# Norms: sums completed by VectorE, four tiles centred and the odd low halves made by GpSimd

## The reference

```
def layer_norm(x, g, b):
    mu = mean(x);  xc = x - mu;  var = mean(xc * xc)
    return xc * rsqrt(var + 1e-5) * g + b

# first block, layer 0 and 1
x = layer_norm(ALPHA * x + 0.5 * swiglu(x, w_in, w_out))      # norms out0, out2
x = layer_norm(ALPHA * x + mix)                               # rg_out (recurrence), o (attention)
x = layer_norm(ALPHA * x + 0.5 * swiglu(x, w_in, w_out))      # norms out1, out3
# second block
h = layer_norm(concat(meta, x))                               # norm emb
h = layer_norm(ALPHA * h + mix);  h = layer_norm(ALPHA * h + swiglu(h))   # mixo0, out4, mixo1, out5
```

## Time and profile before

| | before |
|---|---|
| median of three runs | 1757.0 us (1755.71 to 1757.52) |
| the profiled execution | 1757.72 us, its span 1755.9 us |
| TensorE busy | 1723.1 us (98%), granted clock 0.99 |
| VectorE busy | 1241.3 us (71%) |
| ScalarE busy | 972.5 us (55%) |
| GpSimd busy | 0.2 us, 4 instructions (memsets of one column) |
| DMA, share of the 16 engines | 49.2% |

### The profile page before, as it was taken

The page is one execution under the profiler, slowest core; times in us unless marked ns, Lnnn a source line. Parts: engine busy times, 40 slices in busy tenths (PEclk is TensorE's granted clock), DMA queues, the critical chain, the costliest instruction groups (busy, mean ns, idle before and its releaser), DMA issues.

```text
span 1755.9 us, 33282 instructions
## 1 busy us (share of the span) xinstructions
PE 1723.1 (98%) x11772; PEld 1566.7 (89%) x11772; DVE 1241.3 (71%) x2175; ACT 972.5 (55%) x1700; POOL 0.2 (0%) x4
## 2 busy tenths in 40 slices
PE   8999998999999999999899999999999999999998
PEld 7888998888899888888788888989999999898887
DVE  6776789777664776677787766868665567787765
ACT  5564596655455655466565544565534346665543
POOL 0000000000000000000000000000000000000000
PEclk9999999999999999999999999999999999999999
DMA  6555355455544656533265563334455534345562
GB/s 225 191 201 194 132 181 181 143 186 200 192 142 157 202 186 218 162 116 123 87 217 191 184 213 133 101 117 132 148 175 188 184 114 132 115 145 191 191 203 85
DMA packets 76349, 288.80 MB, mean 164 GB/s; under 512 B 9312, under 2 KB 11616, under 8 KB 76256
## 3 DMA queue, kind: packets, MB, share of 16 engines
q1 hardware_dynamic: 76256, 287.53, 49.2%
HBM read 286.45 MB, written 1.05 MB: 164 GB/s over the span
## 4 chain that ended last, share of the span: by engine, by line
PE 92%; DVE 5%; ACT 2%; issue 1%; DMA 0%; SPq 0%; ACTq 0%; DVEq 0%
PE psum L526 33%; PE psum L527 17%; PE psum L518 12%; PE psum L520 11%; PE psum L519 11%; PE psum L657 1%; PE psum L769 1%; PE psum L604 1%; DVE wlo L1542 1%; PE psum L652 1%; DVE r_sq L1706 1%; ACT whi L1077 1%; PE psum L871 0%; DVE r_sq L1738 0%; PE psum L943 0%
## 5 line engine op out<-in xcount | busy, mean ns | idle before, releaser
L1542 DVE TENSOR_TENSOR wlo<-raw,whi 128x1024 fp32r<-128x1024 f32 (+2 forms) x494 | 640.7, 1305 | 281.2 <-ACT whi L1077 279.9
L526 PE MATMUL psum<-x_split,whi 128*128 128x512 f32 x1760 | 618.4, 395 | 4.3 <-DVE x_split L1577 3.1
L1077 ACT ACTIVATE whi<-raw 128x1024 fp32r<-128x1024 f32 (+2 forms) x494 | 544.8, 1116 | 37.8 <-PE psum L520 18.7
L527 PE MATMUL psum<-x_split,wlo 128*128 128x256 f32 x1760 | 494.5, 281 | 0.0
L526 PEld LDWEIGHTS psum<-x_split,whi 128*128 128x128 f32 x1760 | 331.5, 188 | 82.1 <-DVE x_split L1577 2.8
L518 PE MATMUL psum<-x_split,whi 128*128 128x272 f32 (+1 forms) x1168 | 342.1, 293 | 3.9 <-DVE x_split L1743 3.8
L520 PE MATMUL psum<-x_split,wlo 128*128 128x272 f32 (+1 forms) x1168 | 333.8, 286 | 0.0
L519 PE MATMUL psum<-x_split,whi 128*128 128x272 f32 (+1 forms) x1168 | 332.9, 285 | 0.0
L527 PEld LDWEIGHTS psum<-x_split,wlo 128*128 128x128 f32 x1760 | 331.8, 189 | 0.0
L526 PE MATMUL psum<-h_split,whi 128*128 128x512 f32 x770 | 272.2, 397 | 0.0
L518 PEld LDWEIGHTS psum<-x_split,whi 128*128 128x128 f32 x1168 | 220.2, 189 | 11.4 <-issue 6.3
(11 more groups left out here) (226 smaller groups left out, 1655.7 us busy)
## 6 DMA issues: line engine op xcount, KB each, us to landing
raw<-w_in SPq DMA_DIRECT2D x264, 512.0 KB, 3.3
raw<-w_out SPq DMA_DIRECT2D x96, 704.0 KB, 4.2
raw<-w_mix SPq DMA_DIRECT2D x42, 512.0 KB, 3.3
raw<-w_rg SPq DMA_DIRECT2D x25, 512.0 KB, 3.8
raw<-w_q SPq DMA_DIRECT2D x24, 512.0 KB, 3.3
raw<-w_kv SPq DMA_DIRECT2D x16, 512.0 KB, 3.3
raw<-w_mixo SPq DMA_DIRECT2D x16, 512.0 KB, 3.2
raw<-w_rg_out SPq DMA_DIRECT2D x8, 640.0 KB, 3.9
```

What stands on the lines that cost most here:

```text
L526: nc.tensor.matmul(ps[:, bank, :], whi[slot][:, w], split, start=start, stop=False)
L527: return nc.tensor.matmul(part(bank, 0), wlo[slot][:, w], split[:, 0], start=False, stop=stop)
L1077: nc.scalar.activation(whi[slot][:, 0:cols], raw[slot][:, 0:cols], ACT.Copy).then_inc(w_hi_done, count)
L1542: V.tensor_tensor(wlo[slot][:, 0:cols], raw[slot][:, 0:cols], f(whi[slot][:, 0:cols]), ALU.subtract).then_inc(w_lo_done, 1)
```

## The change

The sums. VectorE itself adds the eighth tile, first its values and then its squares (two instructions of T columns), so that `sums` is complete; TensorE makes the means from `sums` alone, half as many matmuls of both kinds. The low half of the third chunk, which VectorE made at this place, is GpSimd's now. TensorE fills with seven matmuls while the sums are completed. The mean's square no longer waits for the mean of the squares.

The centring. TensorE makes the mean a second time (PSUM bank 3), ScalarE copies it to SBUF (`prod`), and GpSimd centres tiles 4 and 5, then 6 and 7 from that copy. VectorE keeps 0 to 3.

The low halves. VectorE makes those of the even tiles. For an odd tile ScalarE writes the shifted value a second time, unrounded, into `sq`, and GpSimd subtracts the high half from it. `first_chunks` waits for one semaphore or the other by turns. In norm emb only this last part applies.

The one-column Sqrt with its table load moves from the end of the stage to its last four chunks or its fifth.

```diff
@@ -552,3 +560,7 @@
             for k in range(KD):
-                pe.wait_ge(x_ready, KD * x_of[st.name] + k + 1)
+                others = KD // 2 * (x_of[st.name] - 1) + k // 2 + 1
+                if k % 2:
+                    pe.wait_ge(x_odd_ready, others)
+                else:
+                    pe.wait_ge(x_ready, KD + others)
                 for j in range(FIRST):
...
@@ -669,18 +679,22 @@
                     pe.wait_ge(sq_done, KD * n + k + 1)
-                    token_means(sq[:, k, :], 4)
+                    token_means(sq[:, k, :], 5, k == 0, False)
                 pe.wait_ge(emb_squares, 1)
-                ins = token_means(sums[:, 1, :], 4, True)
+                ins = token_means(sums[:, 1, :], 5, False)
             else:
-                pe.wait_ge(sums_done, norm_stages.index(name) + 1)
-                means(sums[:, 0, :], first=True)
-                token_means(sums[:, 0, :], 0)
-                token_means(sums[:, 1, :], 4)
-                pe.wait_ge(acc_free, by_name[name].u0 + by_name[name].units)
-                means(r[:, KD - 1, :], last=True).then_inc(mean_done, 1)
-                token_means(r[:, KD - 1, :], 0)
-                pe.wait_ge(sq_done, KD * (n + 1))
-                ins = token_means(sq[:, KD - 1, :], 4, True)
+                ns = norm_stages.index(name)
+                pe.wait_ge(ax_shifted, (KD - 1) * (ns + 1))
+                keep_warm(7)
+                pe.wait_ge(values_summed, ns + 1)
+                means(sums[:, 0, :], True, True).then_inc(mean_done, 1)
+                token_means(sums[:, 0, :], 2).then_inc(value_means, 1)
+                pe.wait_ge(squares_summed, ns + 1)
+                ins = token_means(sums[:, 1, :], 5)
             ins.then_inc(stat_done, 1)
-            keep_warm(6)
+            if name == "emb":
+                keep_warm(6)
+            else:
+                nc.tensor.matmul(acc(3, T), ones_d, sums[:, 0, t], start=True, stop=True).then_inc(mean_again, 1)
+                keep_warm(3)
             pe.wait_ge(rstd_done, n + 1)
@@ -691,2 +705,5 @@
             keep_warm(12)
+            if name != "emb":
+                pe.wait_ge(mean_copied, norm_stages.index(name) + 1)
@@ -1061,2 +1078,28 @@
+    @block.gpsimd
+    def _(pool):
+        for name in norm_stages:
+            if by_name[name].next:
+                n, slot, _, cols = ahead(by_name[name].next, 0, 0)
+                pool.wait_ge(w_lo_done, n)
+                pool.wait_ge(w_hi_done, n + 1)
+                nc.gpsimd.tensor_tensor(wlo[slot][:, 0:cols], raw[slot][:, 0:cols], whi[slot][:, 0:cols].bitcast(fp32),
+                                        ALU.subtract).then_inc(w_lo_done, 1)
+            T = tokens[name]
+            t = slice(tok0(T), TOK)
+            odd = "emb" if name == "out3" else name
+            pool.wait_ge(mean_copied, norm_stages.index(name) + 1)
+            for k in (4, 6):
+                mean = prod[:, 0, t].unsqueeze(1).broadcast_to([P, 2, T])
+                nc.gpsimd.tensor_tensor(r[:, k:k + 2, t], r[:, k:k + 2, t], mean, ALU.subtract).then_inc(pool_centred, 1)
+            if odd in version:
+                T = norms[norm_no[odd]][1]
+                t = slice(tok0(T), TOK)
+                for k in range(1, KD, 2):
+                    pool.wait_ge(x_hi_done, KD * version[odd] + k + 1)
+                    pool.wait_ge(odd_moved, KD // 2 * (version[odd] - 1) + k // 2 + 1)
+                    nc.gpsimd.tensor_tensor(x_lo[:, k, t], sq[:, k, t], x_hi[:, k, t].bitcast(fp32),
+                                            ALU.subtract).then_inc(x_odd_ready, 1)
     @block.scalar
@@ -1104,5 +1147,8 @@
-        def before_norm(st):
+        def root_table():
             nc.scalar.activation(spare[:, :], eps[:, :], ACT.Sqrt)
+        def before_norm(st):
             if st.next:
@@ -1166,2 +1212,4 @@
                 round_ahead(so, i, j)
+                if isinstance(i, int) and SLOTS * i + j == so.chunks - SLOTS:
+                    root_table()
                 if j % 2:
@@ -1189,2 +1237,4 @@
                 round_ahead(st, i, j)
+                if m == SLOTS:
+                    root_table()
                 if m:
@@ -1206,12 +1256,15 @@
                 for k in range(KD):
-                    act.wait_ge(xc_done, 4 * n + k // 2 + 1)
+                    act.wait_ge(xc_done, xc_before(n) + k // 2 + 1)
                     nc.scalar.activation(sq[:, k, :], r[:, k, :], ACT.Square).then_inc(sq_done, 1)
-            act.wait_ge(stat_done, n + 1)
             if name == "emb":
-                nc.scalar.activation(std_t[:, 0:nt], ps[:, 5, 4:4 + nt], ACT.Sqrt, bias=eps[:, 0:1]).then_inc(std_done, 1)
+                act.wait_ge(stat_done, n + 1)
+                nc.scalar.activation(std_t[:, 0:nt], ps[:, 5, 0:nt], ACT.Sqrt, bias=eps[:, 0:1]).then_inc(std_done, 1)
             else:
                 ns = norm_stages.index(name)
-                nc.scalar.activation(msq[:, 0:nt], ps[:, 5, 0:nt], ACT.Square).then_inc(msq_done, 1)
+                act.wait_ge(value_means, ns + 1)
+                nc.scalar.activation(msq[:, 0:nt], ps[:, 2, 0:nt], ACT.Square).then_inc(msq_done, 1)
                 act.wait_ge(var_ready, ns + 1)
                 nc.scalar.activation(std_t[:, 0:nt], var_t[:, 0:nt], ACT.Sqrt, bias=eps[:, 0:1]).then_inc(std_done, 1)
+                act.wait_ge(mean_again, ns + 1)
+                nc.scalar.activation(prod[:, 0, t], acc(3, T), ACT.Copy).then_inc(mean_copied, 1)
             nxt = None if name == "out3" else by_name["out3" if name == "emb" else name].next
@@ -1224,2 +1277,4 @@
                     nc.scalar.activation(x_hi[:, k, t], r[:, k, t], ACT.Identity, bias=b(k)).then_inc(x_hi_done, 1)
+                    if k % 2:
+                        nc.scalar.activation(sq[:, k, t], r[:, k, t], ACT.Identity, bias=b(k)).then_inc(odd_moved, 1)
                 else:
@@ -1671,5 +1726,3 @@
                 dve.wait_ge(sq_done, i + (KD * norm_no[st.name] + j))
-                ins = V.tensor_tensor(sums[:, :, t], sums[:, :, t], r_sq[:, :, i + (j - 1), t], ALU.add)
-                if last:
-                    ins.then_inc(sums_done, 1)
+                V.tensor_tensor(sums[:, :, t], sums[:, :, t], r_sq[:, :, i + (j - 1), t], ALU.add)
@@ -1685,5 +1738,8 @@
                 V.tensor_copy(sums[:, :, t], r_sq[:, :, 0, t])
-            if last and st.next:
+            if last:
-                rest_of_chunk(*ahead(st.next, 0, 0))
+                dve.wait_ge(acc_free, st.u0 + st.units)
+                V.tensor_tensor(sums[:, 0, t], sums[:, 0, t], r[:, m, t], ALU.add).then_inc(values_summed, 1)
+                dve.wait_ge(sq_done, KD * (norm_no[st.name] + 1))
+                V.tensor_tensor(sums[:, 1, t], sums[:, 1, t], sq[:, m, t], ALU.add).then_inc(squares_summed, 1)
@@ -1722,3 +1778,4 @@
                 dve.wait_ge(msq_done, ns + 1)
-                V.tensor_tensor(var_t[:, 0:nt], ps[:, 5, 4:4 + nt], msq[:, 0:nt], ALU.subtract).then_inc(var_ready, 1)
+                dve.wait_ge(stat_done, n + 1)
+                V.tensor_tensor(var_t[:, 0:nt], ps[:, 5, 0:nt], msq[:, 0:nt], ALU.subtract).then_inc(var_ready, 1)
             dve.wait_ge(std_done, n + 1)
@@ -1727,11 +1784,8 @@
                 centre(2)
-                centre(4)
             dve.wait_ge(spread, n + 1)
-            dve.wait_ge(xc_done, 4 * n + 3)
+            dve.wait_ge(xc_done, xc_before(n + 1))
             v = version.get(name, 0)
             for k in range(KD + 1):
-                if k == 2 and name != "emb":
-                    centre(6)
-                if k == 6:
-                    dve.wait_ge(xc_done, 4 * n + 4)
+                if k in (4, 6) and name != "emb":
+                    dve.wait_ge(pool_centred, 2 * norm_stages.index(name) + k // 2 - 1)
                 if k < KD:
@@ -1739,3 +1793,3 @@
                                            acc(6, T), ALU.mult, ALU.mult).then_inc(xn_done, 1)
-                if k and kind == "x":
+                if k % 2 and kind == "x":
                     c = C_B + KD * n + k - 1
@@ -1747,2 +1801,4 @@
                 if nxt:
+                    dve.wait_ge(w_lo_done, nxt.n0 + 3)
                     rest_of_chunk(*ahead(nxt, 0, 1))
```

20 lines of the change are left out of this document (13 added, 7 removed).

## The result

| | before | after |
|---|---|---|
| median | 1757.0 us (1755.36 to 1758.13, 9 runs) | 1761.8 us (1759.93 to 1763.41, 9 runs) |
| the profiled execution | 1757.72 us, its span 1755.9 us | 1762.68 us, its span 1760.9 us |
| TensorE busy | 1723.1 us | 1718.5 us, granted clock 0.99 |
| VectorE busy | 1241.3 us | 1231.0 us |
| ScalarE busy | 972.5 us | 987.6 us |

The ratio is 1.0029 (95% interval 1.0021 to 1.0037): slower, by 4.8 us. I had forecast 1743, faster. The rival B, an exclusion of VectorE and GpSimd, had 1762.

A forecast was written before the change was run, and what follows sets the result against it. Behind the norms, head and loop were taken as bound by the norm's own chain and VectorE's pace. Norm gains of 15.2 us, less 1.2 for GpSimd hand-overs, gave 14.0 off: 1743 us, range 1737 to 1762.

The forecast's parts named there:

- rival B: VectorE and GpSimd exclude each other when both read two operands in SBUF: +5 us, 1762; chance 0.37.
- GpSimd's chunk low half leaves VectorE for nothing here: Head behind out0: moving this subtraction to GpSimd changes nothing, since it stood in VectorE's wait for the mean.
- The reciprocal at 3.3: Behind out0: reciprocal 3.3 us after the last product's start, before 3.59.
- The first scaling at 4.25: Behind out0: first scaling 4.25 us after the last product's start, before 5.06; later than 4.4 means the head was misread.
- The first product at 5.9: Behind out0: next stage's first product 5.9 us after the last product's start, before 6.75.
- The loop 6.2 to 6.4: Behind out0: the stretch in which eight tiles arrive takes 6.2 to 6.4 us, before 6.73.
- The circle: In the loop: low half, scaling, rounding, low half with two hand-overs, the longest path, 1.45 us per pair of tiles.
- GpSimd's price: In centrings and odd low halves: 2.6 ns a column from the scan, 1.34 us per pair of tiles, 0.67 per tile.
- C: No change, about 1757 us: no exclusion, but GpSimd at about 4 ns a column, so the loop's loss eats the head's gain; chance 0.16.
- The statistics of 272 tokens: Behind mixo0 and out4: twelve of 24 one-column matmuls gone, 1.3 us less about 0.3; those norms gain 2.2 and 2.4.
- Out5: Norm out5, without halves: scaling 0.81 us earlier and the centring behind it gone, taken as 1.15 us gained.

The follow-up runs named there:

- The probe: Kernel before, with GpSimd instructions and overlapping VectorE ones appended behind its end: VectorE's 256-column SBUF subtraction 2.54 us against 0.42 with a PSUM operand; kernel time meaningless.
- the kernels with the early copy: Changed kernel, chunk low halves at norm's end behind an added wait, mean copied from the first mean's bank: 1750.7 us; all tile low halves on VectorE: 1748.3.
- the split kernel: Against the 1748.3 us kernel (mean copied early, all low halves on VectorE): in seven stages 512 third-chunk columns moved into VectorE's wait for the mean; 1744.6 us, 0.9933.

## Why the prediction was wrong

**The step that failed** is "GpSimd's chunk low half leaves VectorE for nothing here", and behind it the choice that GpSimd's instructions run beside VectorE's at no cost to either. In its place the runs showed an exclusion: the chunk's low half holds VectorE's sums (2.65 us for 0.69 behind out0, 2.12 for 0.42 behind o), and the kernel is 8.3 us faster with it off GpSimd; VectorE's chunk work holds GpSimd's last odd low half (1.30 for 0.73), and the kernel is 5.4 us faster without that hold. I had the rule in hand and gave it 0.37. What spoke against it was only that no row showed GpSimd at work; that is no evidence, and the difference between operands in SBUF and in PSUM was readable in every row of VectorE. The Trainium skill has it right (SBUF — State Buffer, section "Who interferes with whom"): two SBUF inputs of VectorE against a read of GpSimd, held for the whole instruction. The probe agrees: 2.54 us against 0.42.

**Point by point.**
- The reciprocal at 3.3: 3.75 after. With the chunk's low half off GpSimd 3.37. The step was right but for GpSimd.
- The first scaling at 4.25: 4.72 after (201.67). 0.38 of it is the late sums (3.75 against 3.37); the spread stays last, as I had it.
- The first product at 5.9: 7.13. Of the 1.2 us, 0.38 is the late sums, 0.72 the first low half held by the second centring. In the kernels with the early copy it is 6.26, with 0.23 of it for the wait ahead of the first centring.
- The loop 6.2 to 6.4: 6.81. The circle was well estimated: 6.25 once the last odd low half is not held.
- GpSimd's price, 1.34 and 0.67 us from the scan: 1.26 and 0.72 alone. C, which wanted 4 ns a column, is out. The Trainium skill's 4497 ns for 2048 columns (GPSIMD Engine Reference, section 3.1) fits the runs: 0.72, 1.26 and 2.34 us for 256, 512 and 1024 lie on a line of 0.18 us and 2.11 ns a column, which gives 4.50 there.
- The statistics of 272 tokens: behind out4 the clock is 1.00 instead of 0.67, and 1.2 came in although the last low half was held; 2.44 in the split kernel, where I had 2.4.
- Out5: 1.04 to the end of the span, where I had 1.15.
- Rival B: three norms +0.8 (measured 0.46), rg_out +1.3 (0.84), mixo1 and o +1.8 (2.30, 2.46), mixo0 +0.9 (0.46), out4 and emb -0.7 together, out3 and out5 -2.3. Its sum of +5 was right, but by luck as to its terms, of which three were not: I had the chunk's low half end before the last product behind out0 to out2, without harm, but it holds the last addition of 512 columns and so that of the eighth tile (0.40); I had not seen that VectorE's chunk work holds GpSimd's last low half (0.56 in each of nine norms); and I had each even low half of the loop meet an odd one, 0.35 per pair, but behind out0 only the first is held, and the others keep 0.48 to 0.49.

**The accounting.** From the changed kernel's 1761.8 us, the holds are undone one at a time: the added wait at the end of the loop gives 5.4 us (1756.4), the chunk back on VectorE 8.3 (1753.5). They do not add: with both it is 1755.3, where the third chunk's low half is late. With the centrings early and the chunk divided 1744.6 is reached, 12 less than before and next to the forecast's 14 less; that the two are so close is in part luck, since behind o 1.23 came in for 2.0 and behind out3 with emb 1.80 for 1.45, at granted clocks of 0.79 and 0.91. So the gain that I forecast was there to be had, from the shorter head and the centrings of GpSimd, and the change as written put some of each of GpSimd's three tasks beside an instruction of VectorE with two operands in SBUF. What the odd low halves bring, I had too high at any rate: the loop without them is 6.17 and with them, unheld, 6.25.

What stays open: why the granted clock behind o is 1.00 in the kernel without the chunk on GpSimd and 0.79 in the split kernel, whose chain to the reciprocal is 0.2 longer; what makes the clock behind out3 and emb differ from kernel to kernel; and what the moved root table is worth by itself. None of these was tried alone.

## What to carry to other kernels

Before work is given to GpSimd, list for each stretch which VectorE instructions have two operands in SBUF (or are products with a constant; for plain copies the probe points the same way), and put GpSimd's work only beside those that read PSUM; the free time of an engine says nothing about that. When an instruction in a trace takes several times its usual length, look at what GpSimd does in the same stretch: in each such case here the one that started later had been held until the other ended. Compare two versions norm by norm at the same granted clock, not by their medians alone, when they lie within 3 us. And a piece of work that was hidden in a wait needs a new place when the wait is used for something else: the third chunk's low half cost 0.4 to 0.6 us a norm wherever it was left to the end.
